# A four-layer decoder on one core: a token's norm factor applied behind the hybrid mixer's projections instead of ahead of them

## The reference

```python
x = layer_norm(DN_ALPHA * x + moe_swiglu(x, ...), ln2_g, ln2_b)      # end of the first block
h = rms_norm_2(x, norm_mix[0])                                       # x * rsqrt(mean(x*x) + 1e-6) * g
z = h @ w_in + b_in                                                  # 3080 columns: xr, gr, q, k, v, o, i, f
xc = causal_dwconv(x_rg, rg_conv_w, rg_conv_b)                       # then gates and a linear recurrence
qk = silu(causal_dwconv(concat(q, k), ml_conv_w, ml_conv_b))         # then a chunkwise mLSTM with v, i, f
y  = concat(y_rg, sigmoid(o) * rms_norm(hm)) @ w_out
x  = x + y
x  = x + conv_ffn(rms_norm_2(x, norm_ffn[0]), ...)                   # norms with vectors nf0, and np0 behind
```

## Time and profile before

| | us |
|---|---|
| median of 3 runs | 2147.81 |
| lowest and highest | 2145.46, 2149.65 |
| the profiled execution, its own time | 2147.78 |
| its span, first to last instruction | 2146.0 |
| TensorE busy | 2111.7 (98%) |
| VectorE busy | 1744.4 (81%) |
| ScalarE busy | 1369.8 (64%) |
| mean granted TensorE clock | 0.991 |

### The profile page before, as it was taken

The page is one execution under the profiler, slowest core; times in us unless marked ns, Lnnn a source line. Parts: engine busy times, 40 slices in busy tenths (PEclk is TensorE's granted clock), DMA queues, the critical chain, the costliest instruction groups (busy, mean ns, idle before and its releaser), DMA issues.

```text
span 2146.0 us, 30445 instructions
## 1 busy us (share of the span) xinstructions
PE 2111.7 (98%) x12258; PEld 1856.2 (86%) x12258; DVE 1744.4 (81%) x2282; ACT 1369.8 (64%) x1771; POOL 53.8 (3%) x43
## 2 busy tenths in 40 slices
PE   8999999999999999999999999989999999999999
PEld 7889999888888888888888888879899998889997
DVE  5776657779999999999999999978677778868776
ACT  5554536558888888888888888858454445554444
POOL 0020003001000000000000001000000000000000
PEclk9999999989999999999999999999999999999999
DMA  8436653549999999999999999934446546236553
GB/s 305 143 130 224 236 196 133 192 175 387 394 396 395 395 391 389 380 377 385 378 383 370 396 375 377 393 111 149 138 157 203 190 162 196 75 103 214 179 182 118
DMA packets 283603, 561.81 MB, mean 262 GB/s; under 512 B 9036, under 2 KB 114128, under 8 KB 283216
## 3 DMA queue, kind: packets, MB, share of 16 engines
q1 hardware_dynamic: 279024, 540.90, 70.3%
q0 software_dynamic: 3568, 15.74, 1.9%
q10 hardware_dynamic: 864, 3.15, 0.4%
HBM read 552.93 MB, written 10.49 MB: 263 GB/s over the span
## 4 chain that ended last, share of the span: by engine, by line
PE 91%; DVE 6%; DMA 1%; ACT 1%; issue 1%; SPq 0%; DVEq 0%; ACTq 0%
PE psum L423 20%; PE psum L425 20%; PE psum L424 20%; PE psum L417 9%; PE psum L419 9%; PE psum L418 9%; PE psum L1872 1%; DVE wl L406 1%; DMA consts<-in_consts 1%; PE psum L679 0%; PE psum L2695 0%; DMA arena<-scratch 0%; DVE SC L519 0%; PE psum L1848 0%; PE psum L1844 0%
## 5 line engine op out<-in xcount | busy, mean ns | idle before, releaser
L406 DVE TENSOR_TENSOR wl<-raw,wh 128x1024 fp32r<-128x1024 f32 x640 | 769.5, 1230 | 179.3 <-ACT wh L398 173.1
L398 ACT ACTIVATE wh<-raw 128x1024 fp32r<-128x1024 f32 x640 | 659.0, 1050 | 264.0 <-PE psum L419 117.0
L406 DVE TENSOR_TENSOR wl<-arena,wh 128x1024 fp32r<-128x1024 f32 x384 | 456.8, 1222 | 37.7 <-ACT wh L398 30.8
L417 PE MATMUL psum<-xh,wh 128*128 128x256 f32 x1600 | 458.9, 287 | 1.0 <-ACT XT L461 0.4
L398 ACT ACTIVATE wh<-arena 128x1024 fp32r<-128x1024 f32 x384 | 403.7, 1062 | 84.9 <-PE psum L425 84.9
L418 PE MATMUL psum<-xl,wh 128*128 128x256 f32 x1600 | 455.5, 285 | 0.0
L419 PE MATMUL psum<-xh,wl 128*128 128x256 f32 x1600 | 455.4, 285 | 0.0
L423 PE MATMUL psum<-wh,xh 128*128 128x512 f32 (+1 forms) x1136 | 448.1, 394 | 0.6 <-DVE wl L406 0.2
L425 PE MATMUL psum<-wh,xl 128*128 128x512 f32 (+1 forms) x1136 | 442.0, 389 | 0.0
L424 PE MATMUL psum<-wl,xh 128*128 128x512 f32 (+1 forms) x1136 | 441.5, 389 | 0.0
L417 PEld LDWEIGHTS psum<-xh,wh 128*128 128x128 f32 x1600 | 309.8, 194 | 6.5 <-DVE wl L406 1.4
(11 more groups left out here) (410 smaller groups left out, 1543.4 us busy)
## 6 DMA issues: line engine op xcount, KB each, us to landing
arena<-in_moe_g SPq DMA_DIRECT2D x72, 1024.0 KB, 9.0
arena<-in_moe_u SPq DMA_DIRECT2D x72, 1024.0 KB, 9.5
raw<-in_moe_d SPq DMA_DIRECT2D x64, 1024.0 KB, 9.4
arena<-in_moe_d SPq DMA_DIRECT2D x48, 1024.0 KB, 8.6
raw<-in_ff_up SPq DMA_DIRECT2D x48, 1024.0 KB, 5.2
raw<-in_moe_g SPq DMA_DIRECT2D x40, 1024.0 KB, 7.9
raw<-in_moe_u SPq DMA_DIRECT2D x40, 1024.0 KB, 9.4
raw<-in_ff_down SPq DMA_DIRECT2D x24, 1024.0 KB, 4.8
```

What stands on the lines that cost most here:

```text
L398: A.activation(unit(s, i)[0], raw_half(s, i), ACT.Copy).then_inc(*s.w_hi.tick(i))
L406: V.tensor_tensor(lo, raw_half(s, i), hi.bitcast(F), SUB).then_inc(*s.w_lo.tick(i))
L417: T.matmul(ps, wh, x[0][:, k, :], start=k == 0, stop=False)
```

## The change

1. The token's factor leaves the turned operand. TensorE transposes X itself, ScalarE and VectorE apply the vector nm0 as a scale of each of eight 128 x 256 chunks when they make the high, low and float32 copies. The factor is computed beside, spread over 128 partitions by TensorE between the third and fourth unit of xr (`token_factor`) and kept in RBH. VectorE multiplies each projection out of PSUM by it, two units at a time (`factor`), into SBUF, where ScalarE adds the bias; v and the gate inputs get it as a scalar of the operation that adds their bias.
2. The vectors nf0 and np0 no longer come by matmuls: GpSimd writes them to DRAM rows early (`pool_gains`), ScalarE's queue reads them back over all partitions. The nine fillers and 48 vector matmuls give way to 20 fillers and three groups of three.
3. TensorE, ScalarE and SP no longer wait for "end" before they branch; the wait is inside the skipped body. ScalarE and VectorE make the mixer's first two units ahead of their last steps of the experts.

```diff
@@ -2122,65 +2129,90 @@
     def again(eng, body):
-        eng.wait_ge(*dve.of("end"))
         with eng.If(second[eng.engine] == 1):
+            eng.wait_ge(*dve.of("end"))
             body()
             eng.wait_ge(*more.dve.of("end"))
+    def again_act(last):
+        at, hi, made = act.n, main.w_hi.n, main.hi_at
+        with A.If(second[A.engine] == 1):
+            last()
+            act_experts(more)()
+            A.wait_ge(*more.dve.of("end"))
+            hi_to(main, un["hy.xr0"][1] + 1)
+        act.n, main.w_hi.n, main.hi_at = at, hi, made
+        with A.Else():
+            hi_to(main, un["hy.xr0"][1] + 1)
+            last()
     def again_dve(last):
-        at = dve.n
+        at, lo, made = dve.n, main.w_lo.n, main.lo_at
         with V.If(second[V.engine] == 1):
             last()
             dve_experts(more, CAP)()
             V.wait_ge(*more.dve.of("end"))
-        dve.n = at
+            lo_to(main, un["hy.xr0"][1] + 1)
+        dve.n, main.w_lo.n, main.lo_at = at, lo, made
         with V.Else():
+            lo_to(main, un["hy.xr0"][1] + 1)
             last()
     N2 = SC[:, 0:48].rearrange("p (t n) -> p t n", t=2)
-    NM0, NM0D = flat(XT[:, 0:4, :]), ar(2048, 2, 128)
+    RBH, BIF = ar(14080, 256), ar(13920, 8)
+    def nm0_turned(k):
+        return bk(4 + k // 2)[:, k % 2 * 256:k % 2 * 256 + 256]
     def pe_out():
-        pe_vector("nm0", 2)
-        pe_vector("nf0", 0)
-        pe_vector("np0", 1)
-        hold_clock(7, 9)
-        Z = ar(0, 2, 1024)
+        hold_clock(2, 20)
         for b in range(2):
             for t in range(2):
...
-                ps = take(4 + 2 * t + b)
-                T.wait_ge(*dve.of(f"nm0.z{t}{b}"))
-                T.wait_ge(*dve.of("nm0.d"))
-                for k in range(4):
-                    x = T.matmul(ps[:, k * P:(k + 1) * P], Z[:, t, (4 * b + k) * P:(4 * b + k + 1) * P], NM0D[:, t, :],
-                                 start=True, stop=True)
+                if t == 0:
+                    claim(2 + b)
+                T.wait_ge(*dve.of(f"moln.X{t}{b}"))
+                for k in range(4 * b, 4 * b + 4):
+                    x = T.transpose(nm0_turned(k)[:, t * P:(t + 1) * P], X[:, t, k * P:(k + 1) * P], ident)
                 x.then_inc(*pe.tick(f"nm0.T{t}{b}"))
-                empties(4 + 2 * t + b, (dve, f"nm0.x{t}{b}"), (act, f"nm0.k{t}{b}"))
+                if t:
+                    drained(2 + b, (dve, f"nm0.x{4 * b + 3}"), (act, f"nm0.k{4 * b + 3}"))
+                if (b, t) != (1, 1):
+                    hold_clock(2, 3)
     def act_out():
-        act_vector("nm0", 2, NM0)
-        for t in range(2):
-            for h in range(2):
-                act_square("nm0", ar(8192, 2, 1024), t, h, of(dve, "moln.X"))
-        hi_to(main, un["hy.xr0"][1] + 1)
-        act_vector("nf0", 0, GAIN["nf0"])
-        act_vector("np0", 1, GAIN["np0"])
-        for b in range(2):
+        g = S("nm0")
+        def square(t, h):
+            act_square("nm0", ar(8192, 2, 1024), t, h, of(dve, "moln.X"))
+        def high(b):
             for t in range(2):
                 A.wait_ge(*pe.of(f"nm0.T{t}{b}"))
-                A.activation(XH[:, 4 * b:4 * b + 4, t * P:(t + 1) * P], heads(bk(4 + 2 * t + b), 4), ACT.Copy
-                             ).then_inc(*act.tick(f"nm0.h{t}{b}"))
-        for b in range(2):
-            for t in range(2):
-                A.wait_ge(*dve.of(f"nm0.x{t}{b}"))
-                A.activation(XT[:, 4 * b:4 * b + 4, t * P:(t + 1) * P], heads(bk(4 + 2 * t + b), 4), ACT.Copy
-                             ).then_inc(*act.tick(f"nm0.k{t}{b}", "nm0.k"))
+            for k in range(4 * b, 4 * b + 4):
+                A.activation(XH[:, k, :], nm0_turned(k), ACT.Copy, scale=g[:, k:k + 1]).then_inc(*act.tick(f"nm0.h{k}"))
+        hi_to(main, un["hy.xr0"][0] + NU)
+        square(0, 0)
+        square(1, 0)
+        high(0)
+        square(0, 1)
+        high(1)
+        square(1, 1)
+        A.wait_ge(*gain_rows.of("all"))
+        for n in range(2):
+            A.dma_start(LG[:, n, :], VD[n].partition_broadcast(P)).then_inc(*ln_in.tick("gains"))
+        for k in range(8):
+            A.wait_ge(*dve.of(f"nm0.x{k | 1}"))
+            A.activation(XT[:, k, :], nm0_turned(k), ACT.Copy, scale=g[:, k:k + 1]).then_inc(*act.tick(f"nm0.k{k}", "nm0.k"))
     def dve_out():
         var, y, x1, hv, v = (N2[:, :, n] for n in (13, 14, 15, 16, 20))
+        g = S("nm0")
         V.wait_ge(*dve.of("end"))
         for t in range(2):
...
+        for t, h in ((0, 0), (1, 0), (0, 1), (1, 1)):
             c = slice(h * 512, (h + 1) * 512)
             x = half(X, t, h)
             V.scalar_tensor_tensor(x, half(ACC, t, h), N2[:, t, 12:13], LG[:, 0, c], SUB, MUL).then_inc(*dve.tick())
             V.wait_ge(*dve.last())
             V.scalar_tensor_tensor(x, x, N2[:, t, 14:15], LG[:, 1, c], MUL, ADD).then_inc(*dve.tick(f"moln.X{t}{h}"))
-        V.wait_ge(*act.of("nm0.v"))
-        V.wait_ge(*dve.last())
-        for h in range(2):
-            for t in range(2):
-                dve_gain("nm0", ar(0, 2, 1024), t, h, NM0)
+        for k in range(8):
+            V.wait_ge(*act.of(f"nm0.h{k | 1}"))
+            V.scalar_tensor_tensor(XL[:, k, :], nm0_turned(k), g[:, k:k + 1], XH[:, k, :].bitcast(F), MUL, SUB
+                                   ).then_inc(*dve.tick(f"nm0.x{k}"))
+        lo_to(main, un["hy.xr0"][0] + 4)
         for t in range(2):
             V.wait_ge(*act.of(f"nm0.sq{t}"))
         V.scalar_tensor_tensor(v, N2[:, :, 18], 1e-6, N2[:, :, 19], ADD, ADD).then_inc(*dve.tick())
         rsqrt(y, v, x1, hv)
-        V.wait_ge(*dve.last())
-        for t in range(2):
-            V.tensor_scalar(NM0D[:, t, :], ident, N2[:, t, 14:15], None, MUL).then_inc(*dve.tick("nm0.d"))
-        lo_to(main, un["hy.xr0"][1] + 1)
-        for b in range(2):
-            for t in range(2):
-                V.wait_ge(*act.of(f"nm0.h{t}{b}"))
-                s = slice(t * P, (t + 1) * P)
-                V.tensor_tensor(XL[:, 4 * b:4 * b + 4, s], heads(bk(4 + 2 * t + b), 4), XH[:, 4 * b:4 * b + 4, s].bitcast(F), SUB
-                                ).then_inc(*dve.tick(f"nm0.x{t}{b}"))
+        dve.name("nm0.r")
...
                 if c < len(between) and between[c]:
                     between[c]()
-            drained(i, (act, f"hy.{name}"))
+            drained(i, (dve, f"hy.{name}f1"))
+        def token_factor():
+            ps = take(2)
+            T.wait_ge(*dve.of("nm0.r"))
+            spread(ps[:, 0:256], N2[:, :, 14:15], 0, 1).then_inc(*pe.tick("nm0.rb"))
+            empties(2, (act, "nm0.rb"))
         def gate_inputs():
...
-                    T.matmul(o, XT[:, k, t * P:(t + 1) * P], wif[:, k, :], start=k == 0, stop=False)
-                x = T.matmul(o, ones[0:4, :], DIF, start=False, stop=True)
+                    T.matmul(o, XT[:, k, t * P:(t + 1) * P], wif[:, k, :], start=k == 0, stop=k == 7)
+            x = T.matmul(ps[:, 16:24], ones[0:4, :], DIF, start=True, stop=True)
             x.then_inc(*pe.tick("hy.if"))
             drained(1, (dve, "hy.ifs"))
...
+        proj(0, "xr", (None, None, token_factor), xw=lambda k: [dve.of(f"nm0.x{k}")])
         gate_inputs()
...
-            A.wait_ge(*pe.of(f"hy.{name}"))
-            for c in cs:
-                A.activation(dst[:, c, :], pair(i)[:, c * 256:(c + 1) * 256], ACT.Identity, bias=bn[:, n0 + c:n0 + c + 1]
+        def proj(name, dst, n0, p):
+            A.wait_ge(*dve.of(f"hy.{name}f{p}"))
+            for c in (2 * p, 2 * p + 1):
+                A.activation(dst[:, c, :], dst[:, c, :], ACT.Identity, bias=bn[:, n0 + c:n0 + c + 1]
                              ).then_inc(*act.tick(f"hy.{name}"))
-        def conv(i, name, dst, src, n0, w, b, o):
+        def conv(name, dst, src, n0, w, b, o):
             for p in range(2):
-                proj(i, name, src[:, o:o + 4, :], n0, (2 * p, 2 * p + 1))
+                proj(name, src[:, o:o + 4, :], n0, p)
                 A.wait_ge(*act.last())
                 for c in (o + 2 * p, o + 2 * p + 1):
...
         hi_to(main, u0 + 2)
+        A.wait_ge(*pe.of("nm0.rb"))
+        A.activation(RBH, bk(2)[:, 0:256], ACT.Copy).then_inc(*act.tick("nm0.rb"))
         hi_to(main, u0 + 4)
-        conv(0, "xr", XC, XR, 0, rw, S("rcb"), 0)
+        conv("xr", XC, XR, 0, rw, S("rcb"), 0)
...
                                        ).then_inc(*dve.tick(name))
+        def factor(i, name, dst, p):
+            V.wait_ge(*pe.of(("unit", un[f"hy.{name}{p}"][1])))
+            V.tensor_tensor(dst[:, 2 * p:2 * p + 2, :], heads(pair(i)[:, p * 512:(p + 1) * 512], 2),
...
             V.tensor_tensor(DD, DN, DN, MUL).then_inc(*dve.tick("hy.dd"))
+        lo_to(main, u0)
+        V.wait_ge(*act.of("nm0.rb"))
+        factor(0, "xr", XR, 0)
         lo_to(main, u0 + 2)
+        factor(0, "xr", XR, 1)
         lo_to(main, u0 + 4)
         V.wait_ge(*act.of("hy.xrt0"))
         taps(XC[:, 0, :], XR[:, 0, :], rw, 0, "hy.xc")
```

(19 more changed lines are left out.)

42 lines of the change are left out of this document (27 added, 15 removed).

## The result

| | before | after |
|---|---|---|
| median | 2147.74 (11 runs) | 2152.62 (11 runs) |
| lowest and highest | 2145.11, 2149.65 | 2149.34, 2154.88 |
| the profiled execution, its span | 2147.78, 2146.0 | 2153.53, 2151.7 |
| mean granted clock | 0.991 | 0.990 |

The changed kernel is slower by 0.23% (ratio 1.0023, 95% interval 1.0015 to 1.003), 4.9 us. The forecast was 2147.3 us with a range up to 2152.2. The medians and averages further down leave out one run of before_branch (2319 us) and one of waits_filled (9293 us), both far above the rest.

A forecast was written before the change was run, and what follows sets the result against it. Whole kernel bound by TensorE, the changed stretch by VectorE. Seam -4.2, spreading +0.4, mixer waits +3.15 gave -0.65 us, with 0.15 for semaphores -0.5: 2147.3 us; 8-in-10 range 2142.6 to 2152.2.

The forecast's parts named there:

- What bounds the kernel: TensorE bounds the whole kernel; VectorE's chain sets the stretch from experts' end to first mixer projection; after the change, TensorE.
- The branch: Behind the experts: TensorE's branch takes 3.57 us again, but from 1414.5, so TensorE comes back at 1418.05.
- rival B: Clearly slower: TensorE comes back no earlier, code fetch starting only when all is drained; holds end 1431.8; 2152.2 us; chance 0.14.
- The holds: Ahead of the first turn: 20 holds are 40 instructions, 0.221 us start to start, 8.8 us, ending at 1426.9.
- rival A: Slightly slower: the clock drops during the holds, costing 3.0 us more, 2150.2 us; chance 0.24.
- Rival D: Filler does not matter: turns follow X, second unit at 1430.8, part 1 gives 9.1 us, 2142.4 us; chance 0.20 with C.
- Ahead of the end: Units 0 and 1 made by ScalarE and VectorE before the experts' end: 0, at most +0.5 us.
- The vectors by DMA: Feed-forward norm's vectors, written over 1100 us ahead of their reader: 0; up to +1 us if small packets delay weight loads.
- GC and HV: TensorE's mixer waits grow through the factor's products: GC from 1.0 to 2.9 us, HV from 2.0 to 3.2 us.

The follow-up runs named there:

- before_branch: Kernel before, with only the early branch added (TensorE, ScalarE and SP wait for the end inside the skipped body): 2149.5 us.
- waits_filled: Kernel after, with 6 fillers ahead of the spreading that waits for GC and 5 ahead of the weighing that waits for HV: 2150.7 us.
- turn_follows: Kernel after, with 5 fillers ahead of the turn instead of 20 and 1 between two turns instead of 3: 2144.3 us.
- factor_out: Kernel after, with the token's factor left out of the mixer (no spreading, no products) and bias steps from PSUM again: 2149.5 us.
- short_hold: Kernel after, with only the first filler of the turn cut from 20 to 8: 2148.4 us.
- branch_late: Kernel after, with TensorE alone waiting for the end of the experts again before it branches: 2154.8 us.
- branch_filled: As before_branch, with 14 fillers behind the vectors instead of 9: 2147.0 us.
- waits_moved: Kernel after, with the two spreadings behind k swapped and the values weighed behind the second unit of oo instead of the first: 2146.4 us.
- both: Kernel after, with the fillers of turn_follows and the two moved steps of waits_moved: 2138.6 us; run again 2136.5, with two fillers more between the spreadings 2138.5.
- before_waits: Kernel before, with the two moved steps of waits_moved and nothing of the change: 2139.9 us; run again 2142.2 us.
- weigh_later: Kernel after, with only the weighing of the values moved behind the second unit of oo: 2150.1 us.

## Why the prediction was wrong, point by point

**What bounds the kernel: right.** VectorE's chain set the seam of before (before_branch moved TensorE and not the seam), and "what is late next? TensorE" came true.

**The branch: wrong.** "I take the whole 3.57 us again, but from 1414.5" gave a restart 1.7 us behind the end of the experts. It was 3.3 us: the record became 5.36 us long. Branching before the end brought 0.4 us (standstill behind the last matmul 4.5 against 4.8 us), as if the time ran from where TensorE has finished its matmuls and not from where the branch is issued. That comes close to rival B's mechanism, which I had argued away with the early load of the flag; what the engine does in that time no trace shows. Cost: 1.6 us.

**The holds: wrong by the clock.** From their start to the first turn the 40 instructions took 11.2 instead of 8.8 us. This is rival A, with 5.0 us at 1.2 GHz behind the restart where it had 5.9, and 11.8 us in all. I had given it 0.24, because the gap was to shrink to 2.9 us; it stayed 4.5. Whether a gap of 2.9 us would have kept the clock isn't shown: in before_branch TensorE stood still for 3.3 us and restarted at 1.2 GHz as well. Cost: 2.3 us, and 0.2 us behind the last turn. Together 4.1 us, and the seam's gain of 4.2 us was 0.2.

**Rival D: right as a mechanism, though not of this kernel.** I wrote that the filler matters and that a turn following X would put the second unit at 1430.8, 14.5 us behind the end. turn_follows has 15.0 us. The filler was the whole of it, and I had the number in hand without drawing from it that 20 is too many.

**Ahead of the end:** the forecast took 0, at most 0.5 us. From the last product of the experts to the end of the scatter 2.6 us passed before and 3.0 after. VectorE makes the low parts of two units first and then both output halves in one go, so now the first scatter product waits, which before followed the expert's last product at once:

```profile
1410.15 0.50 PE L1863 MATMUL psum<-xh,yl 128*128 128x512 f32 x1 [0.93 <-DVE xl L2067]
```

Cost: 0.4 us, inside its bounds. The vectors by DMA cost nothing that is seen: TensorE's first waits in the feed-forward are 1.2 us in both kernels.

**GC and HV: the mechanism right, the sizes too large.** That the waits grow by the products is borne out by factor_out, in which both are back at 1.0 and 2.0 us. GC's wait was forecast at 2.9 us and is 2.7; HV's at 3.2 and is 2.4. The steps of ScalarE that add the bias from SBUF were taken at 0.13 us more each, from the row of another operation, which scales as well; they took 497 ns against 460, 0.04 us more. The estimate by the fixed terms in the Trainium skill (VectorE: DVE Perf Modes, § The TRN2 errata), 224 cycles from SBUF and 172 from PSUM, was 0.04 us, so here the page was right and my row was the wrong row. The products took 0.68 us as forecast. At full clock the mixer grew by 1.5 us where the terms said 3.55.

**The clock in the mixer: the term that wasn't there.** The sum had no price for what follows a wait. The four traces with after's waits (after, short_hold, turn_follows, branch_late) lost 10.2, 6.8, 8.5 and 10.2 us in the mixer, the four with before's waits (before, factor_out, before_branch, branch_filled) 3.4, 6.8, 8.5 and 3.4, the six with at most 0.8 us of wait (waits_moved, the three of both, the two of before_waits) 6.8, 5.1, 5.1, 5.1, 1.7 and 6.8; the two with one long wait left lost 8.5 each. The means of the three groups are 8.9, 5.5 and 5.1 us, so that the traces with the longer waits lost about 3.4 us more. The column of all runs has the same order (22.4, 19.3 and 17.7 us for the means of the same groups).

One place stands out. In all five traces in which TensorE waited 2.7 us for GC (the four and weigh_later) the clock was at 1.2 GHz for 10.2 us from about the end of that wait; in the twelve others, with a wait of at most 1.0 us there or with filler in it, for at most 6.8 us at that place. And waits_filled shows that work in place of the waits brings some 3 us of clock back. But factor_out has the short waits and lost, over all runs, as much as after (21.1 and 21.3 us), and before_branch, which has nothing of the change but the early branch, lost 20.8. So the long waits can't be the only cause: the early restart of TensorE behind the branch, which all three share, is a rival that no run takes apart from them. Against it as the only cause speaks branch_late, where TensorE does not branch early and 23.7 us were lost.

**The sum again:** -0.2 (seam) + 0.4 (ahead of the end) + 1.5 (mixer at full clock) + 3.4 (clock, from the group means) = 5.1 us, measured 4.9. By all runs it is 2.3 us at full clock and 2.6 us of clock. That the first sum comes so close is partly luck: outside the two stretches the traces differ by several us (the experts ended between 1412.7 and 1417.6 us). The time lies near rival B's 2152.2, and of B only the first half is true: its holds would have ended 15.5 us behind the end and did so at 14.6, while the mixer was worse than in B.

**What stays open.** factor_out has nearly the seam of before and, at full clock, its mixer and its whole time (2127.1 us), and is 1.8 us slower by its medians: all of that is clock (21.1 against 18.7 us lost). before_branch lost 2.1 us more than before. Both restart TensorE earlier than before does; why the clock falls more in them isn't known, and so the clock's cause is shown for the part that filler brings back and open for the rest. And why the early branch lasts 5.36 us in after and 3.89 in before_branch isn't known; a standstill of 4.5 and 3.3 us follows from it.

## What to carry to other kernels

When a chain is shortened, size the filler ahead of the next step anew, and at the clock at which it will run: here the filler, made of work that waits for nothing, cost all of the gain, and cutting it gave 8 us back. A wait of TensorE can cost more than its length: filler in two waits, which won none of their time, brought 2.0 us. Follow a chain to the last place at which TensorE waits for it: a wait removed ahead of that place alone brought nothing by the median, and a wait may exist only because a PSUM bank is reused. Compare the clock over several executions before putting it down to an edit: the span and clock of every run showed that factor_out had won no clock, where one trace of each had promised 3.4 us.

## What the runs showed of the hardware that I had not expected

At the skipped body TensorE stood still for 4.2 to 4.9 us behind its last matmul in fifteen of the seventeen traces, with the branch issued before that matmul's end or behind it (3.2 and 3.3 us in the two that add the early branch to the kernel before); on SP and ScalarE the same branch is on record for 50 ns. With the standstill came a stretch at 1.2 GHz each time, and the same code lost 1.7 us in one execution and 6.8 in another to that clock in a stretch of 105 us, while it agreed to 0.6 us otherwise.
